# A hybrid decoder trunk: the state outputs of the S5 mixer summed by TensorE from four products instead of by GpSimd

## The reference, cut to what matters

```python
x_re = jnp.einsum('bsgi,gpi->bsgp', ug, bb_re)
x_im = jnp.einsum('bsgi,gpi->bsgp', ug, bb_im)
...
_, _, h_re, h_im = lax.associative_scan(combine, (a_re_b, a_im_b, x_re, x_im), axis=1)
y = (jnp.einsum('gip,bsgp->bsgi', c_re, h_re)
     - jnp.einsum('gip,bsgp->bsgi', c_im, h_im)
     + d_skip * ug)
```

## Time and profile before

| | |
|---|---|
| median of 3 runs | 1089.09 us (1087.86 to 1093.8) |
| the profiled execution | 1090.4 us, of which the span of the trace is 1088.7 us |
| TensorE busy, weight loads busy | 982.4 us (90%), 839.3 us (77%) |
| VectorE, ScalarE, GpSimd busy | 772.2, 558.7, 384.2 us |
| mean granted TensorE clock | 0.951 of full speed |
| the stage with the S5 steps, in the first and the second layer | about 93 to 310 and 617 to 830 us after the span's start |

### The profile page before, as it was taken

How to read it: one execution, slowest core, us unless ns; L and a number is a source line. 1 busy time by engine, 2 the same in 40 slices (tenths; PEclk the granted TensorE clock), 3 DMA queues, 4 the chain that set the end, 5 groups by cost and what they waited for, 6 DMA issues and landing times.

```text
span 1088.7 us, 16870 instructions
## 1 busy us (share of the span) xinstructions
PE 982.4 (90%) x6183; PEld 839.3 (77%) x6183; DVE 772.2 (71%) x1342; ACT 558.7 (51%) x891; POOL 384.2 (35%) x333
## 2 busy tenths in 40 slices
PE   4899688879899899999979998899889989999996
PEld 4899456557577799999969995566667779999995
DVE  5864989988566676667864658798866667666665
ACT  6334445375555465555555345456556446555554
POOL 0111465667333065333800116677741401011010
PEclk9898889889899899999999998899989999999999
DMA  8942232224435375555539422323353535555551
GB/s 230 252 142 72 78 117 78 78 78 116 149 124 178 134 216 180 174 189 190 175 99 270 124 97 91 117 78 117 81 151 117 193 116 194 187 182 175 190 194 39
DMA packets 135863, 156.79 MB, mean 144 GB/s; under 512 B 16400, under 2 KB 103032, under 8 KB 135800
## 3 DMA queue, kind: packets, MB, share of 16 engines
q1 hardware_dynamic: 135800, 155.96, 45.8%
HBM read 154.90 MB, written 1.05 MB: 143 GB/s over the span
## 4 chain that ended last, share of the span: by engine, by line
PE 60%; DVE 17%; POOL 12%; issue 6%; ACT 4%; DMA 1%; POOLq 0%; SPq 0%; DVEq 0%; ACTq 0%
PE pj L724 45%; PE bX L724 5%; PE bA L724 4%; DVE wl L1500 4%; PE bB L724 3%; POOL mr L2086 3%; POOL s5a L2086 2%; POOL s5h L2093 2%; POOL s5h L2094 1%; POOL bnat L2078 1%; DVE work L1791 1%; DVE bnat L1834 1%; ACT wh L1221 1%; DVE gate L1516 1%; PE bY L1054 1%
## 5 line engine op out<-in xcount | busy, mean ns | idle before, releaser
L1500 DVE TENSOR_TENSOR wl<-ring,wh 128x1024 fp32r<-128x1024 f32 (+1 forms) x276 | 355.9, 1293 | 170.8 <-ACT wh L1221 169.5
L1221 ACT ACTIVATE wh<-ring 128x1024 fp32r<-128x1024 f32 (+1 forms) x276 | 287.9, 1045 | 273.1 <-PE pj L724 237.3
L724 PE MATMUL pj<-hh,wh 128*128 128x256 f32 x1024 | 298.2, 291 | 11.3 <-DVE wl L1500 8.4
L724 PE MATMUL pj<-hl,wh 128*128 128x256 f32 x1024 | 294.6, 288 | 0.0
L724 PE MATMUL pj<-hh,wl 128*128 128x256 f32 x1024 | 294.4, 287 | 0.0
L724 PEld LDWEIGHTS pj<-hh,wh 128*128 128x128 f32 x1024 | 201.7, 197 | 15.5 <-issue 13.6
L724 PEld LDWEIGHTS pj<-hl,wh 128*128 128x128 f32 x1024 | 201.5, 197 | 1.2 <-issue 0.5
L724 PEld LDWEIGHTS pj<-hh,wl 128*128 128x128 f32 x1024 | 201.5, 197 | 0.0
L724 PE MATMUL pj<-wh,hl 128*128 128x512 f32 (+1 forms) x416 | 176.1, 423 | 14.1 <-ACT gate L1208 5.0
L724 PE MATMUL pj<-wl,hh 128*128 128x512 f32 (+1 forms) x416 | 165.7, 398 | 0.0
L724 PE MATMUL pj<-wh,hh 128*128 128x512 f32 (+1 forms) x416 | 165.2, 397 | 0.0
(11 more groups left out here) (291 smaller groups left out, 1492.6 us busy)
## 6 DMA issues: line engine op xcount, KB each, us to landing
ring<-in_ffn_w_up SPq DMA_DIRECT2D x44, 1024.0 KB, 5.1
ring<-in_w_in SPq DMA_DIRECT2D x40, 1024.0 KB, 5.1
ring<-in_ffn_w_down SPq DMA_DIRECT2D x22, 1024.0 KB, 4.9
ring<-in_w_in SPq DMA_DIRECT2D x16, 512.0 KB, 5.3
ring<-in_w_branch SPq DMA_DIRECT2D x8, 1024.0 KB, 5.1
ring<-in_w_out SPq DMA_DIRECT2D x8, 1024.0 KB, 5.0
ring<-in_w_branch SPq DMA_DIRECT2D x8, 512.0 KB, 6.5
ring<-in_w_in SPq DMA_DIRECT2D x8, 256.0 KB, 4.6
```

Of the source, the lines that this page charges most:

```text
L724: return nc.tensor.matmul(o, a, b, start=start, stop=stop, skip_group_check=True)
L1221: A(dst, src, ACT.Copy).then_inc(w_hi.sem, 1)
L1500: TT(dst, src, hi.bitcast(F32), ALU.subtract).then_inc(w_lo.sem, 1)
```

## The change

GpSimd's subtraction and addition go. TensorE sums the four products itself: real state = (first half of the cosine products) minus (second half of the sine products), and the imaginary state likewise, so that 4 matmuls of a pair become 8, with the same sums in the same bank. One of them needs the negated real output matrix `CN`, which ScalarE writes over `cnat` with one more copy in each layer. As TensorE now reads the products themselves, each must stay until its outputs are done, and there are four buffers in turn: `s5a`, the part of `mr`, and the two halves of `s5h`. VectorE's wait for the states of tile s-2 becomes one for the outputs of pair p-2, from s = 4 on; GpSimd waits for its own tile s-2 before it adds tile s.

```diff
-        s5as = [s5a[:, :, :], mr[:, 0, :].rearrange("p (c t) -> p c t", c=2)]
+        s5as = [s5a[:, :, :], mr[:, 0, :].rearrange("p (c t) -> p c t", c=2),
+                *(s5h[:, 2 * n:2 * n + 2].rearrange("p n c t -> p n (c t)") for n in range(2))]
...
+        CN = cnat[:, :, :, :].rearrange("p c j q -> p (c j q)").rearrange("p (j q) -> p j q", j=JC)
...
                 def s5_outputs(p):
                     pe.wait_ge(h5_ready.sem, h5_ready.at(l, 2 * p + 2))
                     y_bank_free()
-                    for c in range(2):
+                    for c in range(4):
                         for e in range(2):
                             j, r = p // 2, 32 * (2 * p % 4 + e)
-                            ins = nc.tensor.matmul(bY[r:r + 32, 0:T], CL[:, c, j, r:r + 32],
-                                                   s5h[:, (2 * p + e) % 4, c, :], start=c == 0, stop=c == 1,
+                            w = (CL[:, 0], CN, CL[:, 1], CL[:, 1])[c]
+                            n, h = ((0, 0), (1, 1), (1, 0), (0, 1))[c]
+                            ins = nc.tensor.matmul(bY[r:r + 32, 0:T], w[:, j, r:r + 32],
+                                                   s5as[(2 * p + e) % 4][:, n, T * h:T * h + T], start=c == 0, stop=c == 3,
                                                    skip_group_check=True, tile_position=(0, r))
...
+                            if n == 2:
+                                A(CN, src[:, :].rearrange("p (j c) -> p j c", j=JC), ACT.Copy, scale=-1.0)
...
                 def s5_turn(s):
 
                     v.wait_ge(x5_done.sem, x5_done.at(l, s // 2 + 1))
-                    if s >= 2:
-                        v.wait_ge(h5_ready.sem, h5_ready.at(l, s - 1))
+                    if s >= 4:
+                        v.wait_ge(y_done.sem, y_done.at(l, s // 2 - 1))
                     for c in range(2):
-                        ins = TT(halves(s5as[s % 2][:, c, :]), halves(bX[s % 2][:, :]),
+                        ins = TT(halves(s5as[s % 4][:, c, :]), halves(bX[s % 2][:, :]),
...
                 def s5_turn(s):
 
                     g.wait_ge(x5_used.sem, x5_used.at(l, s + 1))
-                    c, n = s5as[s % 2][:, 0, :], s5as[s % 2][:, 1, :]
+                    if s >= 2:
+                        g.wait_ge(h5_ready.sem, h5_ready.at(l, s - 1))
+                    c, n = s5as[s % 4][:, 0, :], s5as[s % 4][:, 1, :]
...
                     for c in range(2):
-                        ins = TT(s5as[s % 2][:, c, :].rearrange("p (m t) -> p m t", m=4), gs,
+                        ins = TT(s5as[s % 4][:, c, :].rearrange("p (m t) -> p m t", m=4), gs,
                                  tab[:, c, s:s + 1, :].broadcast_to([P, 4, P]), ALU.mult)
-                    ins.then_inc(pool_step.sem, pool_step.up())
-                    g.wait_ge(pool_step.sem, pool_step.last())
-                    if s >= 4:
-                        g.wait_ge(y_done.sem, y_done.at(l, s // 2 - 1))
-                    c, n = s5as[s % 2][:, 0, :], s5as[s % 2][:, 1, :]
-                    TT(s5h[:, s % 4, 0, :], c[:, 0:T], n[:, T:2 * T], ALU.subtract)
-                    TT(s5h[:, s % 4, 1, :], c[:, T:2 * T], n[:, 0:T], ALU.add).then_inc(h5_ready.sem, h5_ready.up())
+                    ins.then_inc(h5_ready.sem, h5_ready.up())
```

## The result

The changed kernel takes 1060.39 us (median of 4 runs, 1059.7 to 1061.03), the kernel before, beside it, 1089.16 us (4 runs, 1087.86 to 1093.8). The ratio is 0.9728 with an interval of 0.9699 to 0.9758: 28.8 us less, where 15.2 were forecast. The range began at 1063 and does not hold it. The sign is right; the forecast is about half of what came.

The account below looks back on a forecast made before the run. A chain from engine to engine bounds the two S5 stages, no engine full. Terms of -2.8 and -0.9 before the last third, -4.95 and -6.5 in it, sum to -15.2: 1075.2, or 1074 us against the median; range 1063 to 1087.

Parts of the forecast that it names:

- last third: End of each S5 stage: TensorE becomes the limit; -4.95 us in the first layer, -6.5 in the second.
- The clock: After the last cut TensorE's lower clock cost some 2.3 us a layer; half, 1.15 us, was counted as gained.
- (b): S5 steps before the last third: GpSimd's additions slow VectorE's scans; removing them gains 2.1 us in each layer.
- The port rule: VectorE instructions with two SBUF inputs and GpSimd reads contend for the shared port: 23 us, sum 1055.
- (a): VectorE's wait for `h5_ready` at odd tiles goes: 9.1 us in each layer, some 3.2 before the last third.
- GpSimd's 47 us: 64 GpSimd instructions of about 0.73 us go; most of that time was held worth nothing by itself.
- The even tile's additions: After the even tile's addition GpSimd waits for VectorE's scan anyway, so most of its removal is worth nothing.
- TensorE's 64 matmuls: S5 outputs, 4 more for each of 16 pairs: 16 us at full clock; early outputs +1.9 us, late ones +1.0.
- ScalarE's copies: One more copy a layer, ahead of the exponential the first softmax waits for, on the chain: +0.6 us each.
- more than that: Rival, chance 0.15: waits come off in full, contention and clock gain more, new matmuls mostly fill idle time; about 1061 us.
- The waits only move: Rival, chance 0.12: VectorE, no longer waiting, runs into GpSimd's additions and splits at other moments; about 1084.5 us.
- TensorE is the bound: Rival, chance 0.07: the 64 matmuls are dearer than the 64 additions, each pair's on the chain; about 1095 us.

Follow-up runs that it names:

- four buffers: The kernel before with four buffers in turn, GpSimd still adding in place and TensorE reading the sums as before: 1087.71 us, ratio 1.0006.
- three pairs of kernels: Stage comparisons: changed against half of its new matmuls, before against outputs made twice, four buffers against additions put back: 6.4, 6.6 and 5.5 us.
- one kernel with writes: The changed kernel with three GpSimd writes of zeros of 128x512 a tile where the additions stood, each waited for: 1073.42 us, ratio 0.9848.
- Both halves of the additions: The changed kernel with GpSimd's subtraction and addition as dead work in even tiles alone, 1070.16 us, and in odd tiles alone, 1081.11 us.

## Why the prediction was wrong in size and right in kind

*Right.* The change does what it says: 256 records of outputs, 16 in 1.92 us at full clock (1.0 for 8 was taken twice). The wait for `y_done` that took the place of the old one never shows. TensorE became the limit in the last third, and the forecast for it held within 0.5 us in each layer, part of this by luck (see the clock and the matmuls below). The clock after the last cut rose to 1.00. Nothing changed much from the feed-forward network on (-1.5 us, less than two profiles of one kernel differ there).

*Wrong, step by step:*

- **(b) Contention, taken as 2.1 us a layer, 4.2 in all: this is the step that failed.** It was priced by one meeting of a scan with two additions, three times a layer. With all else as in the changed kernel the additions' reads cost about 20 us (21.7 by the medians, 19.6 in the stages). Two things were missed. The meetings are more than the three a layer that I took: the odd tile's scan runs beside the even tile's additions as a rule, and its passes have a mean of 897 ns over all 32 where 392 is the least (506 when the additions are gone). And the prediction had the number in its rows: 392 to 956 ns within one group called for the mean and the total of the other buffer's group, not for one pair out of the timeline. The port rule that was weighed beside it (64 additions, half of them at 0.73 us, 23 us in place of 4.2) would have given 1055. As a price for contention it is close to what was measured; its total is 5 us too low because the terms around it, (a) above all, did not add.
- **(a) VectorE's waits, 6.4 us of the sum ahead of the last third.** (In the last third their 11.7 us served only to show that TensorE is the limit.) Alone they are all worth 0 by the medians (four buffers, 1.0006) and 2.1 us in the stages. A wait for GpSimd's additions ends when GpSimd has done its queue; with the queue as long as before, the time comes back at the next place where VectorE meets GpSimd. The waits turn into time only together with the additions' removal. To say of GpSimd's 47 us that most is "worth nothing by itself" and to count the waits had it the wrong way round: the additions were worth some 20 us by contention and 6 to 14 by their time, and the waits were how part of that showed.
- **The even tile's additions, "after the even tile's addition GpSimd waits for VectorE's scan anyway"**, so that these were costed at nothing: they cost 9.8 us (9.2 in the stages). The cover was real for GpSimd, but not for VectorE, whose scan was the very thing slowed.
- **TensorE's 64 matmuls, 12 us on the chain (1.9 three times, and 1.0 six times in the two last thirds): 3.0 us by the medians, 5.5 to 6.6 in the stages of three pairs of kernels.** Away from the last third they fill idle time in part, and at the one place shown above the output at the lower clock took a stretch that the next matmuls would have spent at that clock. In the last third, where I had 3.0 us a layer, the kernel with half of them is 1.1 and 2.2 us shorter from the fifth output to the eighth.
- **ScalarE's copies, +1.2 us: 0.2 or less.**
- **The clock, half of 2.3 us a layer taken:** it came off in full, since the last wait is 0.5 us. This is inside the last third's 5.3 and 6.1 us; with the full 2.3 that sum would have been 6.1 and 7.65 us, so that its other terms were 0.8 and 1.5 us too high. The forecast also had the clock at this one place only, while in both stages together TensorE's busy time is 8.8 us shorter without the additions than with them, for the same matmuls.

The right case was the rival "more than that", 1061, which had 0.15, with "contention nearer its upper end" in it; it reached the number, though its 18.2 us of waits and 8 us of contention are not how it came about, so that it has the number by luck. "The waits only move" (0.12) describes the four buffers; with the additions kept in the changed kernel it came out 0.6% slower. "TensorE is the bound" is out: half of the matmuls gone gives 3 us, at most some 7.

The shares in order, by kernels: buffers alone 0, matmuls and copies +7.4, additions gone -34.7, together -27.3. The direct comparison is -28.8 in the first set of runs and 0.974, -28.3, in the second. The split between reads and GpSimd's time rests on one kernel with writes, whose GpSimd work is 10 us shorter. Both halves of the additions together cost 4 us more than the sum of the two, which is within the intervals of these ratios (2.0 us more in the stages); nothing more is made of it. Of the 13.6 us that the forecast missed, some 7 are in the S5 stages (22.2 in place of 15.2) and are told by the steps above; for the rest, outside them, the cause stays open.

## What to carry to other kernels

A wait of one engine for another shows where time is lost, not how much a second buffer gives back: if the engine waited for keeps its queue, the wait turns up at the next meeting. Before an instruction of GpSimd is costed at nothing, compare the mean of VectorE's instructions beside it with their shortest, over the whole group; here 32 scan passes had a mean of 897 ns where 392 is the least, and their 27.5 us fell to 14.9 with the additions gone. Sums that a matmul can take into its own accumulation are cheap while TensorE has idle time in that stage: 64 small matmuls, 16 us at full clock, cost 3 to 7 us. And before a price of a few us is read off two medians, compare the stage itself in two profiles: here the rest of the program moved by 8.5 us between two executions of one kernel.

## What the runs showed of the hardware

- A scan pass of 128x128 takes 392 ns at best, and 2.30 us for two passes beside GpSimd's products and additions; a subtraction of 128x512 takes 1480 ns beside additions and 898 without; even an instruction of 128x1 goes from 159 to 292 ns. Writes of zeros by GpSimd in the same places leave these at 949 and 160 ns.
- The granted clock fell to 0.71 for 8 us in one execution, with TensorE busy throughout, and stayed at 1.00 in another of the same program. Between the two S5 stages the same work took 353.0 us at 0.99 and 360.1 us at 0.96.
- TensorE's busy time did not grow with 128 records more (982.4 and 980.5 us in two profiles before, 980.9 after), while its mean granted clock went from 0.951 and 0.954 to 0.972.
- With GpSimd's additions put back, the same 6311 records of TensorE took 999.4 us at a mean granted clock of 0.951: half of the 36.6 us between the spans is busy time, not idle time.
